# Weight preparation ahead of squares and sigmoids, a divided embedding input, and a reordered first pair

## The reference, cut to what matters

```python
x += 0.5 * swiglu(rmsnorm(x), w_gu[0], w_d[0])          # D_FF = 2816
x += mixer(rmsnorm(x))                                  # even layer: DeltaNet + mLSTM; odd layer: gated convolution
x += 0.5 * swiglu(rmsnorm(x), w_gu[1], w_d[1])
x += (p @ w_ple) * sigmoid(rmsnorm(x) @ w_ple_gate)     # the embedding update, p is 256 wide
```

## Time and profile before

| | us |
|---|---|
| median of 3 runs | 2656.34 (2654.22 to 2659.10) |
| the profiled execution, its own time | 2658.97 |
| its span (first to last instruction) | 2657.2 |
| TensorE busy in the span | 2617.2 (98%) |
| VectorE busy | 2129.2 (80%) |
| ScalarE busy | 1185.5 (45%) |
| GpSimd busy | 353.9 (13%) |
| granted TensorE clock, mean | 0.993 |

### The profile page before, as it was taken

One profiled execution on the slowest core, in us unless ns is written; L12 is line 12 of the kernel. 1 busy time (PEld: TensorE's weight loads), 2 busy tenths in 40 slices (PEclk: granted clock), 3 DMA queues, 4 the chain that ended last, 5 costly groups with the idle time before them and its releaser, 6 DMA issues.

```text
span 2657.2 us, 44331 instructions
## 1 busy us (share of the span) xinstructions
PE 2617.2 (98%) x17970; PEld 2581.2 (97%) x17970; DVE 2129.2 (80%) x2630; ACT 1185.5 (45%) x1847; POOL 353.9 (13%) x186
## 2 busy tenths in 40 slices
PE   9999999999999999999999999999999999999998
PEld 9999999999999899999999999999999999999998
DVE  7879786988667679889877998988666789898756
ACT  5535454243222535545444554545411255464545
POOL 2100003332010020000014300000333310000042
PEclk9999999999999799999999999999999999999999
DMA  4223223232002132223232223223222223223231
GB/s 125 80 80 96 80 76 92 56 82 56 17 9 71 47 95 84 80 80 96 80 90 65 80 82 90 84 81 91 84 80 74 72 68 92 80 86 88 75 104 49
DMA packets 404228, 205.63 MB, mean 77 GB/s; under 512 B 18626, under 2 KB 402011, under 8 KB 404024
## 3 DMA queue, kind: packets, MB, share of 16 engines
q1 hardware_dynamic: 403818, 202.72, 26.8%
q10 hardware_dynamic: 206, 0.08, 0.0%
HBM read 195.14 MB, written 7.60 MB: 76 GB/s over the span
## 4 chain that ended last, share of the span: by engine, by line
PE 84%; DVE 12%; ACT 2%; issue 1%; DMA 0%; POOL 0%; DVEq 0%; SPq 0%; ACTq 0%
PE ps L1058 16%; PE ps L1060 16%; PE ps L1059 16%; PE ps L1043 7%; PE ps L1047 7%; PE ps L1044 7%; PE ps L1261 3%; PE ps L1118 2%; PE ps L1117 2%; PE ps L1116 2%; PE ps L1287 2%; DVE ct L3344 1%; DVE r L2655 1%; DVE ct L3341 1%; DVE sumsq L2569 1%
## 5 line engine op out<-in xcount | busy, mean ns | idle before, releaser
L991 POOL TENSOR_TENSOR wlo<-raw,whi 128x1024 fp32r<-128x1024 f32 (+2 forms) x150 | 339.6, 2266 | 2264.4 <-ACT whi L1839 2264.4
L1058 PE MATMUL ps<-tau_hi,whi 128*128 128x320 f32 x1280 | 395.8, 309 | 3.2 <-ACT sq L2060 3.1
L1060 PE MATMUL ps<-tau_hi,wlo 128*128 128x320 f32 x1280 | 395.5, 309 | 0.0
L1059 PE MATMUL ps<-tau_lo,whi 128*128 128x320 f32 x1280 | 395.5, 309 | 0.0
L1850 ACT CAST whi<-raw 128x512 fp32r<-128x512 f32 (+4 forms) x368 | 258.3, 714 | 189.7 <-PE ps L1060 187.8
L1043 PE MATMUL ps<-xh,whi 128*128 128x320 f32 x1040 | 317.6, 313 | 6.3 <-POOL wlo L991 5.5
L1044 PE MATMUL ps<-xl,whi 128*128 128x320 f32 x1040 | 312.9, 309 | 0.0
L2480 DVE TENSOR_TENSOR wlo<-raw,whi 128x512 fp32r<-128x512 f32 (+4 forms) x368 | 289.4, 801 | 17.5 <-ACT whi L1850 17.1
L1043 PE MATMUL ps<-hh,whi 128*128 128x320 f32 x928 | 281.6, 311 | 2.8 <-POOL wlo L991 1.8
L1044 PE MATMUL ps<-hl,whi 128*128 128x320 f32 x928 | 279.4, 309 | 0.0
L2480 DVE TENSOR_TENSOR wlo<-wsum,whi 128x1536 fp32r<-128x1536 f32 (+2 forms) x112 | 180.8, 1614 | 84.1 <-ACT whi L1850 82.7
(11 more groups left out here) (509 smaller groups left out, 6206.6 us busy)
## 6 DMA issues: line engine op xcount, KB each, us to landing
raw<-in_ffn_w_gu SPq DMA_DIRECT2D x320, 256.0 KB, 3.8
raw<-in_ffn_w_d SPq DMA_DIRECT2D x96, 192.0 KB, 3.0
raw<-in_w_in_even SPq DMA_DIRECT2D x32, 512.0 KB, 4.1
raw<-in_ffn_w_d SPq DMA_DIRECT2D x32, 384.0 KB, 3.7
raw<-in_w_in_odd SPq DMA_DIRECT2D x24, 512.0 KB, 3.8
raw<-in_ffn_w_gu SPq DMA_DIRECT2D x16, 512.0 KB, 3.8
raw<-in_ffn_w_d SPq DMA_DIRECT2D x64, 128.0 KB, 2.7
raw<-in_w_ple_gate SPq DMA_DIRECT2D x16, 512.0 KB, 4.3
```

What stands on the lines that cost most here:

```text
L991: pool.tensor_tensor(ring(wlo, n), raw[:, slot, 0:kt, :], ring(whi, n).bitcast(fp32), ALU.subtract).then_inc(lo_ready, 1)
L1058: pe.matmul(out, whi[:, w], hi(i), start=(start and i == 0), stop=False, skip_group_check=True)
L1059: pe.matmul(out, whi[:, w], lo(i), start=False, stop=False, skip_group_check=True)
L1060: last = pe.matmul(out, wlo[:, w], hi(i), start=False, stop=(i == kt - 1), skip_group_check=True)
```

## The change

It has five parts.

1. **Down stages, ScalarE.** The block at the start is prepared two ahead; in the loop it is then the block three ahead, not two, that is prepared before tile `o`'s square. Where no embedding follows, the last call (`o` = 7) is dropped, so the same blocks are prepared as before.
2. **Down stages with `pT`, VectorE.** The first tile of `p` is copied at `o` = 1, the second at `o` = 2.
3. **Embedding stages, ScalarE.** In a gate step the block three ahead is prepared before the sigmoid. In layer 0 the sigmoid of gate 0 comes after the step of emb 2.
4. **Opening, VectorE.** `sums_13` of pair 0 goes ahead of a `tau_rest`; the low part of group 1 goes ahead of `sums_4` and of the scaling of gate 3; the low part of hidden tile 2 goes behind the weights.
5. **Opening, ScalarE.** Groups 0 and 1 of pair 0 are rounded earlier; the activation of gate 3 and groups 2 and 3 go behind the first copy out of PSUM of the pair.

TensorE's and SyncE's programs are the same row for row.

```diff
@@ -2115,14 +2115,11 @@
                         high(1)
                         gate(2)
                         prep(g0 + 7)
+                        prep_pair(p0, 0)
                         tau_round(t, 3)
                         high(2)
-                        prep_pair(p0, 0)
+                        prep_pair(p0, 1)
                         taus_high(0)
-                        gate(3)
-                        prep_pair(p0, 1)
-                        prep_pair(p0, 2)
-                        prep_pair(p0, 3)
                     elif s["plain"] == 2:
                         prep(s["g0"] + 2)
                         norm_root(s)
@@ -2150,6 +2147,10 @@
                         def gate_and_weights():
                             if q > s["plain"]:
                                 gate(q - 1)
+                            elif q > 2:
+                                gate(q - 1)
+                                prep_pair(p, 2)
+                                prep_pair(p, 3)
                             if more:
                                 prep_pair(p + 1, 0)
                             else:
@@ -2197,10 +2198,10 @@
                             for g in [(1,), (1, 4, 2, 3), (1, 4, 2, 3), (1, 2, 3)][d]:
                                 prep_pair(p + 1, g)
                 elif kind == "down":
+                    prep_next(s["n0"], 2)
                     for o in range(KD):
-                        prep_next(s["n0"] + o, 2)
-                        if "pT" in s and o == KD - 1:
-                            prep_next(s["n0"] + KD, 2)
+                        if o + 3 < KD + 2 or "pT" in s:
+                            prep_next(s["n0"] + o, 3)
                         if s["last"]:
                             produce(s["prod"], o, s["g"])
                         if s["tau"] is not None:
@@ -2421,7 +2422,13 @@
                         if s["y"] and o > Y_LAG:
                             y_copy(s, o - Y_LAG - 1)
 
-                    open_gate = None
+                    open_gate = waiting = None
+
+                    def sigmoid_of(o):
+
+                        act.wait_ge(gate_in, s["act0"] + o + 1)
+                        act.activation(hf[:], gt[:], ACT.Sigmoid).then_inc(act_out, 1)
+
                     for at_, (what, o) in enumerate(s["order"]):
                         n = s["n0"] + at_
                         if s["y"] and at_ >= 2 * KD - 2:
@@ -2432,14 +2439,19 @@
                             act.wait_ge(job_done, done_at(j))
                             own(act.copy(halves(sig[:, o, :]), ps[j % 4][:, :, 0:HT]).then_inc(emb_copied, 1), emb_copied)
                             act.sem_inc(slot_free[j % 4], 1)
+                            ahead_of(n)
+                            if waiting is not None:
+                                sigmoid_of(waiting)
+                                open_gate, waiting = waiting, None
                         else:
                             if o == 0:
                                 norm_root(s)
-
-                            act.wait_ge(gate_in, s["act0"] + o + 1)
-                            act.activation(hf[:], gt[:], ACT.Sigmoid).then_inc(act_out, 1)
+                            ahead_of(n)
+                            if o == 0 and s["order"][at_ + 1][0] == "emb":
+                                waiting = o
+                                continue
+                            sigmoid_of(o)
                             open_gate = o
-                        ahead_of(n)
                         if open_gate is not None and (what == "emb" or at_ + 1 == 2 * KD or s["order"][at_ + 1][0] == "gate"):
                             finish(open_gate)
                             open_gate = None
@@ -3177,15 +3189,15 @@
                         hidden_low(1)
                         tau_sums_alone(3)
                         plain_hidden(2)
+                        first = sums_13(p0)
                         tau_rest(t, 2)
-                        first = sums_13(p0)
-                        hidden_low(2)
                         sums_2(p0, first)
                         pair_low(p0, 0)
                         tau_rest(t, 3)
+                        pair_low(p0, 1)
+                        hidden_low(2)
                         sums_4(p0)
                         plain_gate(3)
-                        pair_low(p0, 1)
                         taus_low(0)
 
                     def plain_twice():
@@ -3302,8 +3314,8 @@
                             elif o:
                                 tau_rest(s["tau"], o // 2 - 1)
                         pair_ahead(s["n0"] + o)
-                        if o == 1 and "pT" in s:
-                            for q, j in enumerate(s["pT"]):
+                        if "pT" in s and 0 < o <= KP:
+                            for q, j in [(o - 1, s["pT"][o - 1])]:
                                 done(j)
                                 for c, z in ((0, slice(0, SEQ)), (1, slice(SEQ, T))):
                                     w = z.stop - z.start
```

## The result

The changed kernel takes 2663.93 us (median of 22 runs, 2658.88 to 2668.95) where the kernel before, run beside it, takes 2657.80 (22 runs, 2654.22 to 2661.15). The ratio is 1.0022, with an interval of 1.0016 to 1.0029: it is slower by 4.3 to 7.7 us. The predicted time of 2659.7 is 4.2 us too low; the measured one lies in the range of 2651.5 to 2665.0. Of the 4.2 us, 1.5 are the base (2656.34 from 3 runs, 2657.80 from 22) and 2.7 the change: +3.4 us forecast, +6.1 measured. The direction was right, the size was not. With 0.23% the result also lies just outside the 0.2% within which I had put most of the chance (0.52); it falls to "slower by over 0.2%", which had 0.30.

The account below looks back on a forecast made before the run. The prediction took TensorE to bound the kernel, with 40 us idle. Its terms, -2.7 + 3.1 + 3.1 + 0 - 0.1 + 0 = +3.4 us on 2656.34, gave 2659.7 us (+0.13%), range 2651.5 to 2665.0.

Parts of the forecast that it names:

- The opening, -2.7: Opening: pair 0 starts at 75.0, third product without a wait, fifth waits 1.4 us; -2.7 us, bounds -4.3 and 0.
- First feed-forward to mixer, +3.1 each: Both layers: late first square and GpSimd delay VectorE, TensorE waits in the mixer's first block; +3.1 us each.
- the prediction's first premise: Whole kernel: bound by TensorE, so only what changes its 40 us of idle time can change the time.
- The reading of the port: First feed-forwards: GpSimd's low part holds VectorE's first sum, a copy with one input, until 420.25.
- my lower bound (+1.0 without the port): First feed-forward to mixer, each layer: VectorE keeps the port, only the late square counts, less 0.6 and slack; +1.0 us.
- The mixer outputs, 0: Two mixer output stages: earlier rounding delays the square by 0.1 us; term 0, bounds -0.4 and +1.0 together.
- Layer 0's embedding stage, -0.1: Second feed-forward and embedding, layer 0: -2.2 gained, then VectorE cannot follow, 2.1 on top; -0.1 us, bounds -3.0 and +1.3.
- the stall at n0+5: Layer 0's second feed-forward: TensorE's 1.28 us wait goes because the rounding no longer stands behind the square.
- Layer 1's embedding stage, 0: Second feed-forward and embedding, layer 1: the 0.54 goes, the fourth emb waits 0.5 longer; 0, bounds -1.6 and +1.0.
- A: Rival, whole kernel: the waits simply go and nothing is late in their place; -6.2 us, 2650.1; chance 0.18.
- B: Rival, entries to embedding stages: GpSimd's parts meet VectorE's additions, the port bounds; +7.6 us, 2663.9; chance 0.30 with upper bounds.
- C: Rival, second feed-forwards: roundings come no earlier, their term is 0, sum +3.5 us; forecast with C has 0.52.

Follow-up runs that it names:

- the run with GpSimd held back: Changed kernel, but GpSimd's low part of block n0+3 in the two first feed-forwards waits for VectorE's xl of tile 0; 2662.63 us, one run.
- the run with gate 4 and later as before: Changed kernel, but in both embedding stages the rounding goes ahead of the sigmoid only for gates 0 to 3; 2658.33 us, one run.
- the run with the square first: Changed kernel, but block n0+3 is rounded behind tile 0's square in the two first feed-forwards; 2655.71 us (11 runs), ratio to before 0.9997.
- The split alone: Kernel before, with only the two tiles of p handled behind tiles 1 and 2 of the second feed-forwards; 2660.05 us, one run.

## Why the prediction was right, and where it was wrong

**The opening, -2.7: right, and not the whole of its worth.** -2.55 in the trace. Pair 0 starts at 75.25 (75.0 forecast), the third product doesn't wait, the fifth waits 1.29 (1.4). ScalarE's second copy began at 83.34 behind the roundings that I had named. What I did not count is that at the stall of 3.10 us that it removes the clock falls in a part of the executions, about 1.4 us in the mean by five traces. The row that I read had a granted clock of 1.00, and one trace can't show what happens in others.

**First feed-forward to mixer, +3.1 each: the mechanism right, the price too low.** In the trace of after the first square starts at 415.68; 418.2 was forecast by the clock of before, which is 415.65 with the 2.55 us of the opening taken off. In the same way the first sum ends at 418.05 (forecast 418.05), tile 1's addition at 422.28 (422.35), tile 7's low part at 455.59 (455.65), and TensorE stands for 2.96 and 3.02 us (3.1). What failed is the last step, "TensorE stands for 3.1 us ... and the norm behind it goes with it": I took the time of a stall for its whole cost. It goes back to the prediction's first premise, that only TensorE's 40 us of idle time can change the time: where the clock falls, its busy time grows. Behind both the clock fell, 1.7 us each, and the terms are 4.66 and 4.84, outside my bounds of 1.0 to 3.7. Of the eight stalls of 2.74 to 3.02 us at this place that the runs show, five had the fall. By that count the clock behind the two stalls makes about 2 of the 6 us of the result (1.25 falls of 1.7).

The reading of the port was right where it could be tested: the sum with one input is held (1.54 against 0.49), as the row of 1.78 said. The Trainium skill, "SBUF — State Buffer", section "Who interferes with whom", counts a copy among the instructions that meet GpSimd only where its operands admit a mode with two ports. The trace agrees in so far as this copy is held; in which mode it runs no row here shows. But my lower bound (+1.0 without the port) suggested that the port alone makes 2 us of the term, and the run with GpSimd held back says otherwise: without the meetings at tile 0 the stall is 2.77. VectorE meets GpSimd at tile 1 then.

**The mixer outputs, 0: right** (0.00 in layer 1; in layer 0 the difference between the traces is -4.34 at 950 us and still at 1015, and -4.54 at the stage's end).

**Layer 0's embedding stage, -0.1: right in its size, and in most of its steps.** +0.12 in the trace. The front gain is 2.3 us at gate 2 (-2.2 forecast), made of 1.3 at gate 0 and 1.0 at gate 2. VectorE then can't follow: product and addition of step 5 take 2.88 and 2.91, as forecast, and TensorE waits for the last two low parts (0.60 and 1.50). But GpSimd's two parts are not apart, as I wrote; they stand back to back as before:

```profile
1478.67 5.79 POOL L991 TENSOR_TENSOR wlo<-raw,whi 128x1024 fp32r<-128x1024 f32 x2 [6.78 <-ACT whi L1839]
```

What is new is that the first begins 0.65 us ahead of VectorE's product (1479.32) and so holds it, and the second the addition, where before it began with the product (1486.51, against 1486.48) and the product took 0.82. In the run with gate 4 and later as before they begin together again (1479.71 and 1479.70), and the product takes 0.82.

Here too the clock fell (0.57 from 1497 to 1501), but it cost almost nothing, as it took the place of two waits for VectorE right behind it (0.58 and 0.33 us in the run with the square first, which has no fall there and whose stage comes out at +0.01). One sentence was too narrow: that the rounding's place ends the stall at n0+5. The split alone ends it as well.

**Layer 1's embedding stage, 0: off by 0.75.** I had the fourth emb's wait grow from 1.06 to 1.6; it is 2.30. Its rounding stands behind the last tile's square, which began at 2569.97, where 2569.17 before and the stage's offset of 0.42 make 2569.59: VectorE's last addition came 0.4 us later, and TensorE arrived earlier by the stall of 0.54 that had gone and a little more. The tail's 0.34 us was not in the prediction at all.

**The sum.** Without the core the traces differ by -2.55 + 4.66 + 0.12 + 4.84 + 0.75 + 0.34 and 0.4 behind the last row, that is +8.6, where I had +3.4. Over many executions I estimate the opening at 1.4 more, and the two stalls at 1.25 falls in place of 2 (1.3 less): +5.9, against 6.1 between the medians. That the two agree so well is luck, as five and eight stalls can't give such numbers to within 1 us, and the runs' clocks don't confirm how the sum is made up. By span times (1 - clock), the changed kernel lost 20.9 us in the mean of its 22 runs, against the 15.9 of before (the 21 runs used above): 5.0 more, with a standard error of 0.9, of a difference of 6.1, and only 1.1 (standard error 0.4) is not the clock. The falls counted in the traces (two stalls +2.1, opening -1.4, layer 0's embedding stage +0.4, the entry to layer 1's +0.7) make 1.8 of the 5.0. A part of that time costs nothing, as at the end of layer 0's embedding stage, or in the tail, where TensorE mostly waits and the traces of before and after lost 2.7 and 4.1. Whether the two stalls bring a fall more often than five times in eight, or the core or the tail lose more, stays open.

Of the rivals, A is refuted: the waits don't simply go. B had the right side, and its time (2663.9) is the measured one by coincidence, for its cause is not what the traces show: no meeting at the entries to the embedding stages makes it. In layer 0's embedding stage the meetings only took back what had been gained (+0.12), and layer 1's wait goes with an earlier rounding. The loss is in my own two terms and the clock behind them. C is refuted: the roundings do come earlier, by the 2.3 us at gate 2.

## What to carry to other kernels

Before an instruction that may have to wait for a place is put ahead of others on the same engine, look for who waits for those: here one rounding of 0.8 us, put ahead of a square that VectorE needs, cost 3 us on each of two paths with 0.3 us of slack. Where the place is free anyway, the same move gained. A stall of TensorE can cost more than its length (here 1.7 us more behind five of eight stalls of 3 us), so price it with the granted clock of the window behind it, from more than one trace. And compare traces by stages, by the start of the same instruction, as the span also holds what the clock did elsewhere.

## What the runs showed of the hardware

- TensorE's granted clock falls to its lower level at some stalls and not at others of the same length. Of the thirteen traces, between opening and tail and with the core left aside: at 0.24 to 1.10 us before the mixers never (4 stalls), at 1.49 and 1.50 (end of layer 0's embedding stage) once of four, at 1.88 and at 1.92 once of one each, at 2.30 to 2.67 (layer 1's entry) twice of six, at 2.74 to 3.02 five times of eight, at 3.09 and 3.10 (opening) three times of five, at 3.66 once of one. No fall stands anywhere else there. The falls begin between 1.2 us before TensorE's next matmul and 1.3 us after it.
- A fall takes 1.7 us of full clock; in the opening it was one such step in one trace and two in two. It costs that much time where TensorE goes on without a wait. The double ones of the opening, which began inside the stall, cost 2.80 and 2.53 us, and the one at the end of layer 0's embedding stage about 0.1.
- The times of the executions look like such steps, though that is not shown: the 22 runs of the kernel before lie in groups near 2654.2, 2656.1, 2657.7, 2659.1 and 2661.2, some 1.4 to 2 us apart.
- A VectorE copy with one SBUF input (128x640, fp32) takes 0.49 us alone and 1.54 us beside GpSimd's low part. Which of VectorE's instructions meets GpSimd goes by the order in time: with GpSimd held back, the sum and `xl` of tile 0 were free and those of tile 1 took 1.52 and 2.40.
